# Sixteen more tokens gathered row by row, and the rounding of weighted activations moved to ScalarE, in a two-layer encoder with product-key experts

## What is computed

```python
def peer_ffn(xn, w_query, sub_keys, expert_u, expert_v):
    # in blocks of 128 tokens
    q = (xb @ w_query).reshape(c, PEER_HEADS, 2, HALF_QUERY)
    s = jnp.einsum('chpd,pkd->chpk', q, sub_keys)
    s_top, i_top = lax.top_k(s, PEER_TOPK)
    ...
    best, pos = lax.top_k(cand..., PEER_TOPK)
    g = jax.nn.softmax(best.astype(jnp.float32), axis=-1)
    u = jnp.take(expert_u, idx, axis=0)
    act = jax.nn.gelu(jnp.einsum('chkd,cd->chk', u, xb), approximate=False)
    vsel = jnp.take(expert_v, idx, axis=0)
    return jnp.einsum('chk,chkd->cd', g * act, vsel)
```

## Time and profile before

| | us |
|---|---|
| median of three runs | 3374.58 |
| span of the profiled execution | 3373.7 |
| mixer of layer 1 (to 440) | 440 |
| sorting of layer 1 (440 to 615) | 175 |
| gate table of layer 1 (615 to 765) | 150 |
| experts of layer 1 (765 to 1696) | 931 |

### The profile page before, as it was taken

How to read it: one execution, slowest core, us unless ns; L and a number is a source line. 1 busy time by engine, 2 the same in 40 slices (tenths; PEclk the granted TensorE clock), 3 DMA queues, 4 the chain that set the end, 5 groups by cost and what they waited for, 6 DMA issues and landing times.

```text
span 3373.7 us, 47104 instructions
## 1 busy us (share of the span) xinstructions
PE 3324.8 (99%) x15910; PEld 2731.1 (81%) x15910; DVE 2556.6 (76%) x5315; ACT 1200.8 (36%) x2089; POOL 1048.1 (31%) x791
## 2 busy tenths in 40 slices
PE   8999999999999999999999999999999999999998
PEld 4458865999889988998854688569989889988987
DVE  4674389887888888888826734998788888888888
ACT  2332224783223233223214322348732332233222
POOL 0000027862333333333300000468433333333333
PEclk9999999999999999999999999999999999999999
DMA  4313323679988888888741134146798888888885
GB/s 125 106 38 94 113 96 118 153 250 355 326 304 305 304 302 304 302 304 308 267 156 38 38 104 154 44 141 184 263 355 313 304 303 302 303 308 311 302 304 202
DMA packets 300118, 750.77 MB, mean 223 GB/s; under 512 B 41277, under 2 KB 160829, under 8 KB 270048
## 3 DMA queue, kind: packets, MB, share of 16 engines
q1 hardware_dynamic: 207808, 480.71, 40.6%
q0 software_dynamic: 92192, 268.54, 24.6%
HBM read 681.86 MB, written 67.17 MB: 222 GB/s over the span
## 4 chain that ended last, share of the span: by engine, by line
PE 84%; DVE 11%; DMA 2%; issue 1%; ACT 1%; SPq 0%; ACTq 0%; DVEq 0%; POOL 0%; POOLq 0%
PE ps L1332 30%; PE ps L1318 22%; PE ps L1118 7%; PE ps L987 5%; PE ps L1265 4%; PE ps L1298 3%; PE ps L1176 3%; PE ps L965 2%; PE ps L1211 2%; DVE TI L2153 1%; DVE TI L2162 1%; DVE PS L2156 1%; PE ps L1097 1%; PE ps L931 1%; DVE TV L2159 1%
## 5 line engine op out<-in xcount | busy, mean ns | idle before, releaser
L866 POOL DMA_INDIRECT ROWS<-v_rows_dram,GIS x256 | 331.3, 1294 | 575.3 <-DVE X L2361 493.7
L866 POOL DMA_INDIRECT ROWS<-u_rows_dram,GIS x256 | 298.8, 1167 | 605.3 <-DVE STG L2345 533.2
L1683 ACT ACTIVATE AC<-ps 128x384 f32<-128x384 f32 x192 | 94.5, 492 | 927.0 <-PE ps L1318 922.3
L1332 PE MATMUL ps<-VHI,WHI 128*128 128x512 f32 x1536 | 414.1, 391 | 4.9 <-DVE WLO L2326 3.5
L1332 PE MATMUL ps<-VLO,WHI 128*128 128x512 f32 x1536 | 414.4, 391 | 0.0
L1332 PE MATMUL ps<-VHI,WLO 128*128 128x512 f32 x1536 | 411.3, 389 | 0.0
L1676 ACT CAST VHI<-VRAW 128x512 fp32r<-128x512 f32 x512 | 286.1, 620 | 328.3 <-PE ps L1332 326.9
L2361 DVE SCALAR_TENSOR_TENSOR X<-ROWS,STG,X 128x1024 f32<-128x1024 f32 x256 | 328.4, 1283 | 21.5 <-DMA ROWS<-v_rows_dram,GIS 9.3
L1332 PEld LDWEIGHTS ps<-VLO,WHI 128*128 128x128 f32 x1536 | 288.2, 188 | 63.4
L1332 PEld LDWEIGHTS ps<-VHI,WLO 128*128 128x128 f32 x1536 | 288.4, 188 | 62.1
L1332 PEld LDWEIGHTS ps<-VHI,WHI 128*128 128x128 f32 x1536 | 285.2, 188 | 54.0 <-DVE WLO L2326 4.6
(11 more groups left out here) (294 smaller groups left out, 5240.8 us busy)
## 6 DMA issues: line engine op xcount, KB each, us to landing
VRAW<-v_dram SPq DMA_DIRECT2D x128, 1024.0 KB
URAW<-ut_dram SPq DMA_DIRECT2D x132, 512.0 KB
URAW<-ut_dram SPq DMA_DIRECT2D x62, 1024.0 KB, 5.6
GT<-g_table SPq DMA_DIRECT2D x62, 768.0 KB
g_table<-GST SPq DMA_DIRECT2D x40, 1024.0 KB
WR<-w_in_dram SPq DMA_DIRECT2D x8, 2048.0 KB, 12.0
WR<-w_in_dram SPq DMA_DIRECT2D x32, 512.0 KB, 5.3
WR<-w_q_dram SPq DMA_DIRECT2D x8, 2048.0 KB, 8.2
```

Of the source, the lines that this page charges most:

```text
L866: pool.indirect_dma_start(out=ROWS[:, k % GR, :], out_offset=None, in_=table, in_offset=bass.IndirectOffsetOnAxis(ap=GIS[:, par, k:k + 1], ...
L1332: last = nc.tensor.matmul(ps[:, 2 + o, :], a[:, par, jj, b * P:(b + 1) * P], c[:, dh, jj, :], start=(first and n == 0), stop=(final and n ...
```

## The change

Sixteen tokens (`EX`), the first of block 0, leave the dense path. Their 16 x 128 picks are spread over the 128 partitions, 8 parts of 16 picks, so that one more gathered row a group covers them: `ROWX`, gathered by POOL at the head of each group, its dot with `XGX` (a copy of the 16 tokens in each of the 8 parts) in the first half, a multiply-add into `ACCX` in the second. At the end PE folds the eight parts into block 0's outputs with `SUMX`, a matrix of ones and zeros, in two matmuls. `XHI`, `XLO`, the early activations and the fresh ones are 368 wide; the weights of the 16 tokens in the down product are zeros.

The buffers for this lie in blocks 1 and 2 of `X`, so these are stored to DRAM (`xd`) before the sorting, and loaded again at the end of the experts. The first chunk of the gate table now has 48 tokens to scatter, in 3 sets of 16 and 8 quarters of 2 picks, where it had 2 sets of 32 and 4 quarters of 4: POOL scatters 48 times a layer instead of 64, and the copies into `SCT` are 24 where they were 8, twice a layer. `spread_picks` copies `XGX`, the row numbers and the gates to the eight parts, 23 transfers.

`WHI` is now written by ACT, in `weigh_high`; `WLO` by DVE in `weigh_low`, with row work in between. The rounding and the rest of V are two instructions of 1024 elements instead of four of 512 each. The load of the positions moves from POOL to SP, and some semaphores are merged.

```diff
+EX = 16
+UP = slice(EX, DT)
+XPARTS = P // EX
+SET_TOKENS = 16
+SETS, QUARTERS = (CB - EX) // SET_TOKENS, P // SET_TOKENS
 QPICKS = TOPK // QUARTERS
-SET_TOKENS = CB // SETS
...
+XR = PICKS // XPARTS // GSTEPS
+GSX = GS + XR
...
-    XHI, _ = sb("XHI", [P, KC, DT], F32R)
-    XLO, _ = sb("XLO", [P, KC, DT], F32R)
-    XG, _ = sb("XG", [P, DM])
-    GG, _ = sb("GG", [P, PICKS])
+    XHI, _ = sb("XHI", [P, KC, DT - EX], F32R)
+    XLO, _ = sb("XLO", [P, KC, DT - EX], F32R)
+    XG, xg_at = sb("XG", [P, DM])
+    ACCX, _ = sb("ACCX", [P, DM], offset=xg_at)
+    ROWX, _ = sb("ROWX", [P, DM], offset=x_at + 4 * DM)
+    IDXX, _ = sb("IDXX", [P, PICKS], I32, offset=x_at + 4 * DM)
+    GATEX, _ = sb("GATEX", [P, PICKS], offset=x_at + 4 * DM + 4 * PICKS)
+    XGX, _ = sb("XGX", [P, DM], offset=x_at + 8 * DM)
+    GG, _ = sb("GG", [P, GSTEPS * GSX])
...
+                        sp.wait_ge(xs_ready, NB + 1)
+                        sp.dma_start(xd, X[:, 1:3, :]).then_inc(zero_stored, 16)
...
                         sp.dma_start(SCT[SET_TOKENS * q:SET_TOKENS * (q + 1), :, s, h0:h1].rearrange("p a h m -> p a (h m)"),
-                                     SCP[SET_TOKENS * s:SET_TOKENS * (s + 1), :, q, h0:h1].rearrange("p a h m -> p a (h m)")
+                                     SCP[EX + SET_TOKENS * s:EX + SET_TOKENS * (s + 1), :, q, h0:h1].rearrange("p a h m -> p a (h m)")
                                      ).then_inc(cells_moved, 16)
+
+                def spread_picks():
+
+                    sp.wait_ge(sel_ready, PICKS_X)
+                    for q in range(1, XPARTS):
+                        sp.dma_start(XGX[EX * q:EX * (q + 1), :], XGX[0:EX, :]).then_inc(picks_here, 16)
+                    n = PICKS // XPARTS
+                    with nc.allow_non_contiguous_dma("a word a step and partition"):
+                        for q in range(XPARTS):
+                            dst = slice(EX * q, EX * (q + 1))
+                            sp.dma_start(GI_X[dst], IDXX[0:EX, n * q:n * (q + 1)].rearrange("p (s k) -> p s k", k=XR)).then_inc(picks_here, 16)
+                            sp.dma_start(GG_X[dst], GATEX[0:EX, n * q:n * (q + 1)].rearrange("p (s k) -> p s k", k=XR)).then_inc(picks_here, 16)
+
+                def reload(i):
+                    sp.dma_start(X[:, 1 + i, :], xd[:, i]).then_inc(x_back, 16)
...
+                spread_picks()
+                sp.wait_ge(zero_stored, 32)
...
+                    pool.wait_ge(rowx_used, s + (before + 1))
+                    pool.nop().then_inc(pool_went, 1)
+                    pool.indirect_dma_start(out=ROWX[:], out_offset=None, in_=table,
+                                            in_offset=bass.IndirectOffsetOnAxis(ap=GIS[:, par, GS:GSX], axis=0)
+                                            ).then_inc(rowx_loaded, 16)
...
-                            last = nc.tensor.matmul(ps[:, bank, 0:DT], a[slot][:, k, :], c[:, k, :],
+                            last = nc.tensor.matmul(ps[:, bank, UP], a[slot][:, k, :], c[:, k, :],
...
+                def add_apart():
+
+                    pe.wait_ge(rowx_used, 2 * GSTEPS + 1)
+                    for dh in range(2):
+                        nc.tensor.matmul(ps[:, 2 + DB * dh, :], SUMX[:], ACCX[:, 512 * dh:512 * dh + 512], start=False, stop=(dh == 0))
...
-                    for jj in (2 * pair, 2 * pair + 1):
-                        nc.scalar.copy(VHI[:, dh, jj, :], VRAW[:, dh, jj, :]).then_inc(v_hi, 1)
+                    two = slice(2 * pair, 2 * pair + 2)
+                    nc.scalar.copy(VHI[:, dh, two, :], VRAW[:, dh, two, :]).then_inc(v_hi, 1)
...
+                def weigh_high(g, par, n, first):
+
+                    jj = JG - 1 if n == 0 else n - 1
+                    if n == 0 and not first:
+                        act.wait_ge(v_out, g * NOUT - (NOUT - 1))
+                    act.wait_ge(wf_ready, g * JG + (n + 1))
+                    nc.scalar.copy(WHI[:, par, jj, :], WF[n % 2]).then_inc(whi_ready, 1)
...
+                    if i == 0:
+                        dve.wait_ge(zero_stored, 32)
+                        nc.vector.scalar_tensor_tensor(XGX[0:EX, :], X[0:EX, 0, :], SR[0:EX, 0:1], GF[0:EX, :],
+                                                       ALU.mult, ALU.mult)
...
+                def row_numbers(tokens, b):
+
+                    first, second = (SEL[tokens, k, b].rearrange("p h m -> p (h m)") for k in range(2))
+                    st.did(nc.vector.scalar_tensor_tensor(GIF[tokens], first, float(NK), second, ALU.mult, ALU.add))
+                    st.then(dve)
+                    st.did(nc.vector.tensor_scalar(GIF[tokens], GIF[tokens], COL[tokens, L_BASE:L_BASE + 1], None, ALU.add))
+                    st.then(dve)
+
+                row_numbers(slice(0, EX), 0)
+                nc.vector.tensor_copy(GATEX[0:EX], SEL[0:EX, 2, 0].rearrange("p h m -> p (h m)"))
+                nc.vector.tensor_copy(IDXX[0:EX], GIF[0:EX]).then_inc(sel_ready, 1)
+                dve.wait_ge(sel_ready, PICKS_X)
+                nc.vector.tensor_copy(GG_OWN, SEL[:, 2, NB - 1].rearrange("p h m -> p (h m)").rearrange(by_step, k=GS))
+                row_numbers(slice(0, P), NB - 1)
+                nc.vector.tensor_copy(GI_OWN, GIF.rearrange(by_step, k=GS))
...
-                    dve.wait_ge(wf_ready, g * JG + (n + 1))
-                    nc.vector.tensor_copy(WHI[:, par, jj, :], WF[n % 2]).then_inc(whi_ready, 1)
+
+                def weigh_low(g, par, n):
+
+                    jj = JG - 1 if n == 0 else n - 1
...
+                def dot_apart(s, par):
+
+                    dve.wait_ge(rowx_loaded, l * ROWX_LAYER + s * 16 + 16)
+                    nc.vector.tensor_tensor_reduce(ROWX[:], ROWX[:], XGX[:], 1.0, 0.0, ALU.mult, ALU.add,
+                                                   accum_out=STG[:, par, GS:GSX]).then_inc(rowx_used, 1)
...
+                    nc.vector.scalar_tensor_tensor(ACCX[:], ROWX[:], STG[:, par, GS:GSX], ACCX[:],
+                                                   ALU.mult, ALU.add).then_inc(rowx_used, 1)
...
+                    dve.wait_ge(v_out, (NG - 1) * NOUT + max(o, DB if b == 0 else 0) + 2)
+                    if b:
+                        dve.wait_ge(x_back, 32)
...
-                        if rows and jj:
-                            for k in ROWS_AT[jj]:
-                                rows(g, par, k)
+                        if columns and jj == 0:
+                            weigh_low(g + 1, 1 - par, 0)
+                        ks = list(ROWS_AT[jj]) if rows else []
+                        behind = len(ks) if jj == 0 else 1
+                        for k in ks[:len(ks) - behind]:
+                            rows(g, par, k)
                         if columns:
                             weigh_fresh(g + 1, 1 - par, jj)
-                        if rows and not jj:
-                            for k in ROWS_AT[jj]:
-                                rows(g, par, k)
+                        if rows and jj == 0:
+                            (dot_apart if rows is dot else add_apart)(g, par)
+                        for k in ks[len(ks) - behind:]:
+                            rows(g, par, k)
+                        if columns:
+                            weigh_low(g + 1, 1 - par, 1 + jj)
```

More of the change, by code:

```diff
@@ L514, in encoder, with token_part @@
     ACT_SQUARES, DVE_SQUARE = (NB - 1, 0, 1), 2
+    def token_part(n):
+        b, half = divmod(n, 2)
+        t0, t1, ks = max(b * P, EX), (b + 1) * P, slice(4 * half, 4 * half + 4)
+        return (slice(None), ks, slice(t0, t1)), (slice(None), ks, slice(t0 - EX, t1 - EX))
     def places_and_columns(k):
@@ L591, in _ @@
             sp.dma_start(ZE[:], zemb).then_inc(mlp_loaded, 16)
+            with nc.allow_non_contiguous_dma("positions are a few words"):
+                sp.dma_start(POSF[:].bitcast(I32), positions.rearrange("(b p) -> p b", p=P)).then_inc(mlp_loaded, 16)
             sp.wait_ge(w2_zero, 1)
@@ L657, in load_pre @@
                 def load_pre(g, slot):
[L658 removed]
+                    sp.dma_start(PREB[:, slot, UP], ed[g, :, UP]).then_inc(pre_loaded[slot], 16)
                 def load_g(g, slot):
@@ L802, in _ @@
             pool.wait_ge(w2_zero, 2)
-            with nc.allow_non_contiguous_dma("positions are a few words"):
-                pool.dma_start(POSF[:].bitcast(I32), positions.rearrange("(b p) -> p b", p=P)).then_inc(pos_loaded, 16)
             pool.memset(FR[HID:P, :, :], 0.0).then_inc(w2_zero, 1)
@@ L1251, in early_up @@
                                 pe.wait_ge(ea_ready, e - (ESLOTS - 1))
-                        last = nc.tensor.matmul(ps[:, GBANKS + ahead % ESLOTS, 0:DT], early_slot(ahead)[:, k * P:(k + 1) * P],
-                                                XN2[:, k, 0:DT], start=(k == 0), stop=(k == KC - 1))
+                        last = nc.tensor.matmul(ps[:, GBANKS + ahead % ESLOTS, UP], early_slot(ahead)[:, k * P:(k + 1) * P],
```

(21 more changed lines are left out.)

144 lines of the change are left out of this document (83 added, 61 removed).

## The result

The changed kernel takes 3398.51 us (median of four runs, 3394.29 to 3400.68); the kernel before took 3374.23 in the same comparison. The ratio is 1.0071, with a 95% interval of 1.0058 to 1.0083. It is slower, as forecast, by 24.3 us instead of 9.

A forecast was written before the change was run, and what follows sets the result against it. PE, busy 99% of the span, was taken to bound the kernel, with SP's queue between it and its weights before the experts. Terms of +3.6 (layer 1) and +5.4 (layer 2), together +9.0, gave 3384 us; range 3346 to 3408.

The forecast's parts named there:

- Part 1, narrower up matmuls: Up matmuls of 368 instead of 384 columns: -13.7 us a layer in the expert stage, -2.0 in the stage before.
- Parts 2 and 3, engines and the extra row, 0: Expert stage: DVE's and ACT's shifted work stays inside a group's slack, one more gathered row fits the DMA engines; 0 each.
- Part 4, entry 11: SP's queue before the experts: 24 transfers of scattered cells, formerly 8, delay early entry 11's load; +7.6 us a layer.
- Part 4, entry 17: Gate table: second 24 transfers plus 23 copies in SP's queue delay entry 17's load, so slot 7 starts late; +10.7 us a layer.
- Part 5, ends: Ends of the layers: two added PE matmuls, less than 1 us together, delay the last outputs; +1.0 in layer 1, +2.8 in the last.
- Rivals A and B: SP's queue: A, both waits covered, 3347 us, chance 0.16; B, only one wait real, 3363 us (or 3369), chance 0.16.

The follow-up runs named there:

- the cells in lots: The changed kernel with its 48 copies of scattered cells a layer issued in small lots behind early entries 7 to 12 and slots 4 to 11: 3346.16 us.

## Why the prediction was right, and where its size was off

The direction and the mechanism were right: the narrower matmuls give what their columns say, and the transfers that the change adds to SP's queue take it back and more. The range held the time near its upper end, and so did the forecast's own, 3372 to 3400; the loss was 24.3 us where 9 were forecast (by the spans 25.2).

- *Part 1, narrower up matmuls*: -13.7 a layer in the experts; measured -12.7 and -13.9. That they lie so close is partly luck: the narrow matmuls alone gave 15.9 and 16.0 in this stretch, since hardly anything of the 1.7 us that I took off for its start was lost, and against them stand PE's two new matmuls, which I had put at the ends, and in layer 1 a longer stall at the last group. The gate table's share of -2.0 is real (-2.6 and -2.4 with the narrow matmuls alone). The Trainium skill (TensorE: Matmul & The Clock Gate, Back-to-back issue gap) had the 31 us at some 10; here a column of work with 24 of these matmuls fell from 9.67 to 9.49 us, some 7 ns each, as the 6.7 ns forecast from the two measured pitches, and the trace disagrees with the page.
- *Parts 2 and 3, engines and the extra row, 0*: right in the middle of the stage, by two runs of their own; DVE's order of work is not quite free at the last group of layer 1 (see the ends).
- *Part 4, entry 11*: ACT's cast ended at 606.89 (forecast 607.9), and DVE's split came at 607.00 (607.9); the stretch cost 8.7 us in layer 1 and 10.6 in layer 2, where 7.6 was the term. Mis-sized by 1.1 and 3.0: the slow start of 1.4 us in layer 1 (ten matmuls, 0.14 each) and 2.5 in layer 2 (eighteen), and a second one of 1.4 at entry 8 in layer 1. The chain itself was 1 us early in layer 1, and the stall 0.5 longer in layer 2.
- *Part 4, entry 17*: this is the step that failed in size. The term was 10.7 us a layer, 8.7 with the gain of the early entries; measured 13.2 and 15.0. The stall was 12.9 and 14.6 us. In it are XGX's 7 copies, 4.41 us where I took 3.4 from the loads at the start, in layer 1 4.5 us from ACT's cast to slot 7 where I took 3.6, and in layer 2 24 copies in 16.93 us where I took 15.6. On top comes the slow start: the 16 matmuls of slot 7 and the 12 behind them took 6.63 us up to the next slot (663.70 to 670.33), where they took 3.86 (642.50 to 646.36): 2.8 us. I had priced a stall at its length.
- *Part 5, ends*: +2.2 and +2.0 for +1.0 and +2.8. PE's two matmuls are dearer than said, 1.31 us and not under 1:

```profile
3374.24 1.88 PE L1399 MATMUL ps<-ACCX,SUMX 128*128 128x512 f32 x4
3375.55 1.50 PE L1390 MATMUL ps<-VHI,WHI 128*128 128x512 f32 x4
```

  In layer 1 DVE was late at the last group, where PE stood 2.13 us and not 0.47; the same is 1.54 us with the cells in lots, 1.55 with the rounding back on DVE and 3.67 without the gathers, so it is neither of these. Nothing here says what else in DVE's new order it is. The two matmuls and this stall lie in the stretch of the down products, not in that of the ends.

Of the missing 16 us, slow starts are 5.6 in layer 1 (1.4 at entry 8, 1.4 at entry 11, 2.8 at slot 7) and 5.1 in layer 2 (2.5 and 2.6), and the longer stalls at slot 7 are 2.2 and 3.9; what is left evens out to within 1 us. Rivals A and B are out: both waits are real, and each can be had alone.

The version to take is the change with the cells in lots: 3346.16 us. It stands 8 us above the narrow matmuls alone. Of these, 1.3 us a layer are PE's two matmuls, 1.3 in layer 1 the stall at the last group, 2 and 0.8 the tails. In the profiled execution 2.8 more are a slow start in the experts of layer 2, behind a stall of 2.76 us; with the narrow matmuls alone a stall of 2.69 us stands there, followed by matmuls at full pace. So part of the 8 us may be chance; the rest was not split up.

## What to carry to other kernels

Count the transfers that a change adds to a queue written out by hand, and for each load behind them compare their issue time with the time by which that load is early: up to there they cost nothing, beyond it about one for one, however few bytes they have. With the 48 copies in lots between the loads the same 71 transfers a layer left no stall of PE that can be put down to them. A long stall of the engine that is never idle costs its length and the slow start behind it.

## What the runs showed of the hardware

- What a transfer costs SP to issue does not follow its bytes: 0.65 us for 1 KB in 16 partitions or 4 KB in 32, 0.63 for 64 KB in 16 (`XGX`), 0.33 to 0.58 for 512 KB in 128 (`URAW`), but 0.86 for some 1.3 KB in 10 or 11 partitions and 0.80 for some 0.7 KB in 5 or 6.
- Behind a stall of 6.8 us or more PE ran at a granted clock of 0.50, which took 1.4 and 2.5 us behind entry 11 and 2.8 and 2.6 behind slot 7; matmuls with no use, issued into the wait, kept it at 1.00. Stalls of 2.4 to 2.8 us were followed by either level.
- The DMA engines took the extra row in stride: 328 GB/s where 310 had been.
